# Gated-delta stage: the triangular inverse grown in 32-row diagonal blocks, two heads to a PSUM bank, and other products placed between a level's two halves

## The reference, cut to what matters

```python
def chunk_gated_delta(q, k, v, g, beta, s0):
    ...
    decay = jnp.cumsum(g, axis=-1)
    dmask = jnp.exp(jnp.where(causal, diff, -jnp.inf))
    k_beta = k * beta[..., None]
    v_beta = v * beta[..., None]
    A = jnp.where(strict, jnp.einsum('bhnid,bhnjd->bhnij', k_beta, k) * dmask, 0.0)
    T = lax.linalg.triangular_solve(eye + A, jnp.broadcast_to(eye, A.shape),
                                    left_side=True, lower=True)
    u = T @ v_beta
    w = T @ (k_beta * jnp.exp(decay)[..., None])
    qk = jnp.einsum('bhnid,bhnjd->bhnij', q, k) * dmask
    ...
    def step(S, inp):
        u_n, w_n, qk_n, qd_n, kd_n, gl_n = inp
        v_new = u_n - w_n @ S
        o_n = qd_n @ S + qk_n @ v_new
        S = S * gl_n[..., None, None] + jnp.einsum('bhck,bhcv->bhkv', kd_n, v_new)
        return S, o_n
```

## Time and profile before

| | |
|---|---|
| median of three runs | 1419.92 us |
| span of the profiled execution, first to last instruction | 1416.3 us |
| TensorE busy, instructions | 1367.1 us (97%), 10652 |
| VectorE busy, instructions | 947.8 us (67%), 1593 |
| ScalarE busy, instructions | 590.5 us (42%), 1455 |
| GpSimd busy, instructions | 568.0 us (40%), 645 |
| mean granted TensorE clock | 0.986 |
| bytes moved | 234.64 MB, 166 GB/s |

### The profile page before, as it was taken

The page is one execution under the profiler, slowest core; times in us unless marked ns, Lnnn a source line. Parts: engine busy times, 40 slices in busy tenths (PEclk is TensorE's granted clock), DMA queues, the critical chain, the costliest instruction groups (busy, mean ns, idle before and its releaser), DMA issues.

```text
span 1416.3 us, 29230 instructions
## 1 busy us (share of the span) xinstructions
PE 1367.1 (97%) x10652; PEld 1244.8 (88%) x10652; DVE 947.8 (67%) x1593; ACT 590.5 (42%) x1455; POOL 568.0 (40%) x645
## 2 busy tenths in 40 slices
PE   6999899989989999999999999999999999999997
PEld 4899899988978888888799999999999997887675
DVE  5527786774366666788879656666665567576388
ACT  6524344345556656625544333333333325443220
POOL 4888867871033334233331443432443434000051
PEclk8999999999999999999999999999999999999999
DMA  9431435334364545432143454554344448997794
GB/s 333 134 106 45 115 98 134 105 89 151 99 216 129 166 136 166 135 128 76 67 106 103 138 174 144 165 187 158 128 155 157 149 153 329 364 371 255 263 325 177
DMA packets 184410, 234.64 MB, mean 166 GB/s; under 512 B 17709, under 2 KB 118641, under 8 KB 184305
## 3 DMA queue, kind: packets, MB, share of 16 engines
q1 hardware_dynamic: 181424, 221.52, 48.4%
q10 hardware_dynamic: 2880, 11.72, 2.1%
HBM read 170.29 MB, written 61.73 MB: 164 GB/s over the span
## 4 chain that ended last, share of the span: by engine, by line
PE 60%; DVE 7%; ACT 4%; issue 3%; POOL 2%; DMA 1%; SPq 0%; POOLq 0%; ACTq 0%; DVEq 0%
PE bank L2354 28%; PE bank L2268 11%; PE bank L305 3%; PE bank L1678 2%; PE bank L1132 2%; PE bank L1141 2%; PE bank L1638 2%; PE bank L2285 1%; PE bank L1143 1%; ACT hp L1728 1%; PE bank L1174 1%; PE bank L1165 1%; ACT vp L1279 1%; PE bank L1092 1%; PE bank L1099 1%
## 5 line engine op out<-in xcount | busy, mean ns | idle before, releaser
L2268 PE MATMUL bank<-split 128*128 128x512 f32 x924 | 212.1, 390 | 2.9 <-DVE split L2401 2.3
L2268 PEld LDWEIGHTS bank<-split 128*128 128x128 f32 x924 | 172.7, 188 | 44.5 <-DVE split L2397 5.7
L2354 PE MATMUL bank<-Tlo,rh 128*128 128x272 f32 x640 | 184.7, 289 | 0.0
L2354 PE MATMUL bank<-Thi,rh 128*128 128x272 f32 x640 | 184.2, 288 | 0.0
L2354 PE MATMUL bank<-Thi,rl 128*128 128x272 f32 x640 | 184.0, 288 | 0.0
L305 PE MATMUL bank<-hT_hi,whi 128*128 128x384 f32 (+1 forms) x504 | 167.0, 331 | 2.0 <-DVE wlo L295 1.8
L305 PE MATMUL bank<-hT_hi,wlo 128*128 128x384 f32 (+1 forms) x504 | 165.2, 328 | 0.0
L305 PE MATMUL bank<-hT_lo,whi 128*128 128x384 f32 (+1 forms) x504 | 165.1, 328 | 0.0
L2354 PE MATMUL bank<-hT_lo,rh 128*128 128x272 f32 x480 | 138.5, 289 | 0.0
L2354 PE MATMUL bank<-hT_hi,rl 128*128 128x272 f32 x480 | 138.4, 288 | 0.0
L2354 PE MATMUL bank<-hT_hi,rh 128*128 128x272 f32 x480 | 137.9, 287 | 0.0
(11 more groups left out here) (450 smaller groups left out, 3358.1 us busy)
## 6 DMA issues: line engine op xcount, KB each, us to landing
wada<-w_ada SPq DMA_DIRECT2D x12, 2048.0 KB, 9.0
raw<-w_up SPq DMA_DIRECT2D x40, 512.0 KB, 5.0
wsum<-w_down SPq DMA_DIRECT2D x11, 1024.0 KB, 5.6
wt<-wsum SPq DMA_DIRECT2D x11, 1024.0 KB, 4.0
rW<-wt SPq DMA_DIRECT2D x44, 256.0 KB, 6.6
split<-split SPq DMA_DIRECT2D x22, 512.0 KB, 4.9
wraw<-w_in SPq DMA_DIRECT2D x21, 512.0 KB, 4.1
rows<-convrow ACTq DMA_DIRECT2D x16, 577.5 KB, 3.7
```

What stands on the lines that cost most here:

```text
L2268: last = pe.matmul(ps[down_bank(q, r)][:], a[:, rows], w, start=(k == 0 and m == 0), stop=(k == KH - 1 and m == 2))
L2354: last = pe.matmul(ps[banks[c]][:, 0:NC], w[:, ks], a, start=(n < 3 and k == 0 and p == 0), stop=(k == 3 and p == 2), skip_group_check=True)
```

## The change

What it does, for the stage's eight full tiles and the last:

- Levels 0 to 3 (LEVELS 2 to 16) work on the four diagonal blocks of 32 rows (ROWS) instead of two of 64. Each P or X step of a head is four products of 32x32 instead of two of 64x64. Xc, Lc, ATc and the masks are half as wide.
- Level 4 (LEVELS 32, named FULL) joins blocks 0 with 1 and 2 with 3 (BELOW), writes into Xf and into a new tile X0u (the inverse of the upper 64 rows). Level 5 (64) is as before, from X0u and Xf.
- Two heads share a bank: pair p = heads 2p, 2p+1 has bank p for P, X and the state's update, and bank 2+p for V; kS of all heads is in bank 2. The copies of P, the adds to X and the copies of V take a pair at a time.
- kS (`read_state`) stands after P of level 0, `right_sides` after grow_X(0). The other products stand between a level's P and its X.
- The scales are split: those from k early, those from q in one instruction, and the last scale of the outputs is computed with one instruction less.
- On VectorE `coupling` stands behind grow_X(5), and `first_blocks`, `first_level`, `later_levels` behind `new_state`.

The diff, cut to its core:

```diff
+B32 = P // 4
+FULL = LEVELS.index(B32)
...
-        lv = lambda t, l, h: (t * LV + l) * HEADS + h
-        top = lambda t: LEVELS.index(DEC_SEQ // 2) if t == PTILES else LV - 1
+        lvp = lambda t, l, p: (t * LV + l) * PAIRS + p
+        top = lambda t: FULL if t == PTILES else LV - 1
+        ROWS = [slice(r * B32, (r + 1) * B32) for r in range(P // B32)]
+        BELOW = ((0, 1), (2, 3))
+        p_at = lambda p, rows, i, n: ps[p][rows, n * i:n * i + n]
+        x_at = lambda p, rows, i, part: ps[p][rows, P + HB * i + B32 * part:P + HB * i + B32 * part + B32]
...
+            def level_P(t, l):
...
+                for p in range(PAIRS):
                     if l:
-                        pe.wait_ge(on["g_X"], lv(t, l - 1, h) + 1)
...
+                        pe.wait_ge(on["g_X"], lvp(t, l - 1, p) + 1)
+                    elif t:
+                        pe.wait_ge(on["g_S"], (t - 1) * HEADS + 2 * p + 2)
+                    for i, h in enumerate((2 * p, 2 * p + 1)):
+                        if l > FULL:
+                            last = pe.matmul(p_at(p, DOWN, i, HB), Lh[x][UP, h, :], X0u[x][UP, h, :], start=True, stop=True)
+                        elif l == FULL:
+                            for a, b in BELOW:
+                                last = pe.matmul(p_at(p, ROWS[b], i, B32), Lq[x][ROWS[a], h, :], Xc[x][ROWS[a], h, 0, :], start=True, stop=True)
+                        else:
+                            for r in ROWS:
+                                last = pe.matmul(p_at(p, r, i, B32), Lc[x][r, l, h, :], Xc[x][r, h, 0, :], start=True, stop=True)
                     last.then_inc(on["g_P"], 1)
...
+            def level_X(t, l):
...
+                            for r in ROWS:
+                                pe.matmul(x_at(p, r, i, 0), Xc[x][r, h, 1, :], Pb[r, h, 0:B32], start=True, stop=True)
+                            for r in ROWS:
+                                last = pe.matmul(x_at(p, r, i, 1), Pb[r, h, 0:B32], Xc[x][r, h, 1, :], start=True, stop=True)
                     last.then_inc(on["g_XX"], 1)
...
-                level(t, 0)
+                level_P(t, 0)
+                read_state(t)
+                level_X(t, 0)
                 if more:
-                    turn_kq(n)
-                level(t, 1)
-                level(t, 2)
+                    turn_k(n)
+                level_P(t, 1)
+                if more:
+                    gram(n, 0)
+                level_X(t, 1)
+                if more:
+                    gram(n, 1)
+                level_P(t, 2)
+                if more:
+                    turn_q(n)
+                level_X(t, 2)
+                level_P(t, 3)
                 if t:
                     turn_o(t - 1)
-                level(t, 3)
+                level_X(t, 3)
+                level_P(t, 4)
+                level_X(t, 4)
                 if more:
-                    scores(n)
-                level(t, 4)
-                if more:
-                    gram(n)
+                    turn_v(n)
+                    level_P(t, 5)
                 if t:
                     ada_columns(t - 1)
                 if more:
-                    level(t, 5)
+                    level_X(t, 5)
+                new_values(t)
+                outputs(t, (0, 1))
+                if more:
                     turn_A(n)
-                    turn_v(n)
-                state(t)
+                outputs(t, (2, 3))
+                if more:
+                    scores(n)
                 if t < PTILES:
                     ada_rows(t)
...
             def keep_P(t, l):
-                rows = DOWN if l == LV - 1 else slice(0, P)
-                for h in range(HEADS):
-                    act.wait_ge(on["g_P"], lv(t, l, h) + 1)
-                    act.activation(Pb[rows, h, 0:HB], ps[h][rows, 0:HB], ACT.Copy).then_inc(on["g_Pb"], 1)
+                rows, n = (DOWN, HB) if l > FULL else (slice(0, P), B32)
+                for p in range(PAIRS):
+                    act.wait_ge(on["g_P"], lvp(t, l, p) + 1)
+                    act.activation(Pb[rows, pair(p), 0:n], ps[p][rows, 0:2 * n].rearrange("p (h c) -> p h c", c=n),
+                                   ACT.Copy).then_inc(on["g_Pb"], 1)
...
                     keep_P(t, 4)
+                    whole_X(t)
+                    keep_P(t, 5)
                     decay_exp(n)
-                    k_decayed(n)
-                    keep_P(t, 5)
-                    whole_X(t)
-                    keep_A(n)
                     v_scaled(n)
                     keep_V(t)
+                    squares_q(n)
+                    keep_A(n)
                     squares_o(t)
+                    decay_row(n)
...
             for t in range(TILES):
+                n = t + 1
                 if t:
                     out_scale(t - 1)
-                if t + 1 < TILES:
-                    scales(t + 1)
-                    q_decayed(t + 1)
-                    causal(t + 1)
+                    q_decayed(t)
+                if n < TILES:
+                    scales_k(n)
+                    causal(n)
+                    scales_q(n)
```

More of the change, by code:

```diff
@@ L1542, in gdn_dve @@
                 grow_X(t, 1)
+                if not more:
+                    wo_low(dve, 1)
+                grow_X(t, 2)
                 if t:
@@ L1545, in gdn_dve @@
                 if not more:
-                    wo_low(dve, 1)
-                grow_X(t, 2)
-                if not more:
                     wo_low(dve, 2)
                 grow_X(t, 3)
+                if more:
+                    upper_X0(t)
                 if t:
```

274 lines of the change are left out of this document (154 added, 120 removed).

## The result

The changed kernel takes 1482.26 us (median of four runs, 1478.7 to 1485.57) against 1420.16 for the kernel before on the same chip: 1.0433 times as long, 95% interval 1.0418 to 1.0449. Forecast were 1406 us, 1394 to 1418, and "faster" with 82%. Sign and size are both wrong.

A forecast was written before the change was run, and what follows sets the result against it. TensorE was taken to bound the full tiles, with the chain of waits through it, and VectorE the last. Terms: -1.4 us a tile, 8 tiles -11, last tile -3; 1419.9 - 14 = 1406 us, range 1394 to 1418.

The forecast's parts named there:

- (1): Levels 0 to 4 of a full tile: 60 steps at 0.0635 us instead of 0.117; -3.2 us a tile.
- (2) to (6): Full tile: round trips between tile shapes, P-to-X and X-to-P waits, VectorE's order, tile's end, next tile's first blocks; +1.8 us.
- (4): VectorE's order in a full tile: turn_o waits for out_rows, +0.3 us; level 4's six copies come late, +0.33.
- (7): Last tile, bounded by VectorE: fewer adds save 0.4 us in each of four levels, right sides 1.4; -3 us.
- A: Every step of levels 0 to 4: four row tiles do not overlap as two do; 1428 us, chance 8%.
- B: TensorE's matmul issue rate is the limit: 29 ns a record, a step 0.23 us; 1488 us, chance 3%.
- C: VectorE and GpSimd hinder each other at a tile's head, grow_X(0) 1.2 us late; 1412 us, chance 12%.
- D: Gain spent on waits priced too low (six copies, hand-overs, nine changes of shape); 1417 us, no change, chance 7%.

The follow-up runs named there:

- the burst: The kernel before with five bursts of useless identity products (128x128, 32x32, 64x64) put behind the last tile; 1550.39 us (one run).
- in the old: The kernel before in its own order, one head a bank, only the products of levels 0 to 3 cut to 32-row blocks; 1465.83 us, ratio 1.0324.
- the order alone: The changed kernel with blocks of 64 rows in place of 32, the rest as changed; 1441.97 us, ratio 1.0163.
- the best version: The kernel before with levels 0 and 3 cut to 32-row blocks in tiles 1 to 6 and the weight load held until level 4's products are done; 1417.12 us.
- the later load alone: The kernel before with nothing but the weight load held until level 4's products are done; 1418.66 us, ratio 0.9989.
- halved products: The kernel before with each 64-row product of levels 0 to 4 made as two of 32 columns; 1568.94 us (one run).

## Why the prediction was wrong, point by point

**(1) Smaller blocks, -3.2 us a tile.** This is the step that failed, not in the price of a product but in what goes with it. The step was 0.06 to 0.08 us as forecast. Left out was what it costs to bring the instructions: the records of these steps double, and TensorE's instructions come in packets of 128 records, each fetched while the block before it runs. The prediction had this term at nothing. At 4 x 0.0635 for 32 records a stretch of steps asks for a packet in about 1 us; the burst got one in 3.5 us, and beside a full DMA it takes longer (the 126 records ahead of the stop that ends at 428.70 had taken 2.7 us, and with the stop 6.0). In place of -26 us the eight tiles and the last got +40 (in the new order) or +46 (in the old): stops, which grew from the order alone (2.8 us) to the changed kernel by some 25 us, and the lower clock (0.98 in the stage with the order alone, 0.74 in the changed kernel). How much of the rest is clock is only bounded: 40 less 25 is 15, plus whatever the smaller products gave back, which the stops hide.

The gain of the smaller products exists. Tiles 1 to 6 of the best version take 21.9 us on the mean (418.29 to 549.61, by six) where the kernel before takes 22.6: 0.7 for two levels. The prediction's price gives 1.3, 12 steps a level at 0.0535 us less. (The expectations put 0.8 a level, the 3.2 us by four; the 60 steps are those of five levels.) The other 0.5 us a tile goes in the main into waits that the kernel before does not have: 1.8 us in the stage in twelve waits for ScalarE's Pb, which the longer products had covered, and 0.8 us in two for the loads into stg.

**(2) to (6), +1.8 us a tile.** The sum is right within what the parts can claim: the order alone costs about 1.9, and 2.0 with the two tiles in which the clock fell. Part of this may be luck: which part has which share was not taken apart, and the copies of level 4 in (4) are not in the kernel that shows it.

**(7) Last tile, -3 us.** Wrong by 8: +5.1 with the order alone, +7.3 in the changed kernel. I had counted VectorE's work and not its order. With two heads to a step TensorE has nothing between a pair's X and the next P, and in the order alone a 1.2 us split (596.48 to 597.70) stands on VectorE between the X that ends at 597.2 and the add for which P waits 1.0 us. The other waits, 0.9 for Pb and 0.8 for Xf, are for ScalarE, which (7) did not look at; the clock is 0.92.

**The rivals.** A fell (four row tiles do overlap). B had 3%, and its time of 1488 us is close, but by a wrong mechanism, so that its nearness is luck: 32 records stand within 0.45 us, which no floor of 29 or 25 ns a record allows; the floor is one per packet. All that I weighed of the rate was single steps (four records in 0.11 us). What I should have asked of the trace is how many records its densest stretches have: in a full tile 126 records in 4.7 us. Doubling them in place could not pass. C did not show: VectorE's masks for the later levels take 0.29 and 0.55 us on the mean. Of D only the last tile's waits came.

The Trainium skill, page "Runtime: NRT & Kernel Launch", section "Instruction fetch mechanics", describes this very mechanism: instructions are streamed in 16 KiB blocks of 256 by a DMA queue that the sequencer drives. Size and count agree with the 13 and 24 packets here. It adds that crossing a block is mostly hidden, since dispatch is slower than the refill. That does not hold for small products: in the burst 1.93 us of work (at the lower clock) and 1.5 us of stop a block. Taken at its word it would have made me leave the cost out too, but its 256 instructions were enough to work out the demand.

The sentence that a stretch at 0.50 would be a cause left out has come true: about 135 us of them.

**What stays open.** Why a packet's start is delayed by 2 us beside one full DMA and by 4 beside another, and why its transfer takes 0.9 us here and 1.35 there in the quiet burst (that difference is most of the one between 3.45 and 4.0). What brings the clock down in the new order where no long stop stands ahead of it. In the best version the tiles say that the cut levels gave most of the gain (tiles 1 to 6 take 22.5 us on the mean with the later load alone, 21.9 with both); the times of the whole kernel hardly tell the two apart. That more than the next packet can be held in reserve shows nowhere: the first packets of a dense stretch pass without a stop since they had landed before it.

## What to carry to other kernels

Cutting a product into smaller ones buys time in the array and pays in instructions: before doing so, count the records of the densest 4 us of TensorE, and keep them, doubled, under some 128 in 3.5 us with quiet DMA, and under 128 in 6 to 7 us beside a bulk load. If idle time has the releaser "issue", look at the distance in records and at the DMA share beside it; move the load to where the products are large. And price each stop with what follows it: 3.4 or 6.8 us at half clock when 64-row and whole products followed, up to 20 (changed kernel) or 41 (halved products) when light ones did.

## What of the hardware was not expected

- TensorE's instructions come in packets of 128 matmul records with their weight loads, one in 3.45 to 4.0 us at a DMA share of 0.02: 1.0 to 1.1 us from a block's first record to the start of the next packet, 0.9 to 1.35 us for its transfer, 1.3 to 1.5 us from its landing to its first product. With the DMA engines full the start came 2.3 to 4.9 us behind, and a packet's records and their stop took 4.7 to 7.3 us.
- Four 32x32 products on four row tiles, each two records, follow the last four by 0.06 to 0.08 us. Two 64x32 products cost as much as two 64x64, 0.117 us.
- Behind a stop of some 3.1 us between 64-row and whole products the clock went from 1.00 to 0.50 in seven of eight cases, and was back after 3.4 us in six and 6.8 in one. Behind the 2.4 us wait at the stage's start it stayed low for 41 us where 32-column products followed.
